# Three fixed expert pairs instead of two at the start of a mixture-of-experts layer

## The reference

```python
hid = silu(einsum('td,edf->tef', t, w_gate)) * einsum('td,edf->tef', t, w_up)
routed = einsum('tef,efd->td', hid * gates[:, :, None], w_down)
shared = (silu(t @ ws_gate) * (t @ ws_up)) @ ws_down
return (routed + shared).reshape(shp)
```

## Time and profile before

| What | Value |
|---|---|
| Time, median of 3 runs (lowest, highest) | 1366.26 us (1365.38, 1369.22) |
| The profiled execution: its time, its span | 1367.02 us, 1365.0 us |
| TensorE matmul busy | 1150.9 us, 84% of the span |
| VectorE, ScalarE busy | 441.6 us (32%), 301.1 us (22%) |
| Bytes moved, mean rate | 497.52 MB, 364 GB/s |
| Mean granted TensorE clock | 0.925 of full |

### The profile page before, as it was taken

One profiled execution on the slowest core, in us unless ns is written; L12 is line 12 of the kernel. 1 busy time (PEld: TensorE's weight loads), 2 busy tenths in 40 slices (PEclk: granted clock), 3 DMA queues, 4 the chain that ended last, 5 costly groups with the idle time before them and its releaser, 6 DMA issues.

```text
span 1365.0 us, 20661 instructions
## 1 busy us (share of the span) xinstructions
PE 1150.9 (84%) x7420; PEld 603.9 (44%) x7420; DVE 441.6 (32%) x1222; ACT 301.1 (22%) x562; POOL 69.3 (5%) x85
## 2 busy tenths in 40 slices
PE   3897988998888886978879998899977888887877
PEld 2675745444333432323348775544423333332323
DVE  0645474222122222212246474631222122212213
ACT  1523532111111111101144355111111111111102
POOL 0220010000000000000033002000000000000000
PEclk8899988999889888989989998999989898898989
DMA  9689586899999999999994947679999999999994
GB/s 364 251 330 399 212 341 247 352 412 421 419 418 417 416 406 422 405 421 420 418 400 143 358 161 309 222 318 413 421 419 416 420 416 415 412 421 420 420 421 166
DMA packets 95526, 497.52 MB, mean 364 GB/s; under 512 B 8752, under 2 KB 8752, under 8 KB 53744
## 3 DMA queue, kind: packets, MB, share of 16 engines
q1 hardware_dynamic: 93632, 491.48, 89.2%
q0 software_dynamic: 1840, 5.31, 1.0%
HBM read 494.14 MB, written 2.62 MB: 364 GB/s over the span
## 4 chain that ended last, share of the span: by engine, by line
PE 58%; DMA 30%; SPq 3%; issue 3%; ACT 2%; DVE 2%; POOL 1%; DVEq 1%; ACTq 0%
PE PS L1006 29%; DMA weights<-in_w_up 27%; PE PS L800 12%; PE PS L1038 4%; PE PS L974 3%; PE PS L945 2%; SPq L412 2%; PE PS L990 2%; DMA weights<-in_w_ada 2%; DMA weights<-in_w_in 1%; PE PS L821 1%; PE PS L967 1%; SPq L452 1%; PE PS L896 1%; PE PS L636 1%
## 5 line engine op out<-in xcount | busy, mean ns | idle before, releaser
L1006 PE MATMUL PS<-weights,gathered 128*32 128x512 f32 (+1 forms) x2624 | 408.9, 685 | 142.3 <-DMA weights<-in_w_up 134.4
L1006 PEld LDWEIGHTS PS<-weights,gathered 128*32 128x32 f32 (+1 forms) x2624 | 118.6, 130 | 428.9 <-issue 335.9
L1719 DVE SCALAR_TENSOR_TENSOR hidden<-PS,slot_gate,silu 128x256 f32<-128x256 f32 x50 | 24.2, 484 | 508.3 <-ACT silu L1254 506.2
L1038 PE MATMUL PS<-weights,hiddenT 128*32 128x512 f32 (+1 forms) x1312 | 182.3, 596 | 0.0
L1254 ACT ACTIVATE silu<-PS 128x256 f32<-128x256 f32 x50 | 19.2, 384 | 535.3 <-PE PS L1006 535.3
L974 PE MATMUL PS<-pick_rows,x_parts 128*128 128x384 f32 (+2 forms) x616 | 121.9, 348 | 6.6 <-DVE pick L1671 6.6
L974 PEld LDWEIGHTS PS<-pick_rows,x_parts 128*128 128x128 f32 x616 | 104.8, 195 | 49.1 <-issue 40.6
L800 PE MATMUL PS<-weights_split,hT_high 128*128 128x512 f32 x448 | 111.8, 405 | 8.1 <-ACT hT_high L1104 6.1
L1267 ACT ACTIVATE y_hi<-PS 128x512 fp32r<-128x512 f32 x100 | 59.7, 597 | 222.2 <-PE PS L1038 222.2
L800 PEld LDWEIGHTS PS<-weights_split,hT_high 128*128 128x128 f32 x448 | 86.0, 195 | 30.4 <-issue 11.8
L1730 DVE TENSOR_TENSOR y_lo<-PS,y_hi 128x512 fp32r<-128x512 f32 x100 | 69.2, 692 | 77.6 <-ACT y_hi L1267 77.6
(11 more groups left out here) (270 smaller groups left out, 912.7 us busy)
## 6 DMA issues: line engine op xcount, KB each, us to landing
weights<-in_w_down SPq DMA_DIRECT2D x128, 1024.0 KB, 11.8
weights<-in_w_gate SPq DMA_DIRECT2D x96, 1024.0 KB, 10.4
weights<-in_w_up SPq DMA_DIRECT2D x96, 1024.0 KB, 12.4
weights<-in_w_ada SPq DMA_DIRECT2D x24, 2048.0 KB, 13.3
weights<-in_w_gate SPq DMA_DIRECT2D x64, 512.0 KB, 7.0
weights<-in_w_up SPq DMA_DIRECT2D x64, 512.0 KB, 8.0
weights<-in_w_in SPq DMA_DIRECT2D x9, 2048.0 KB, 11.2
weights<-in_w_out SPq DMA_DIRECT2D x4, 2048.0 KB, 15.7
```

The costliest lines, as they stand in the source:

```text
L1006: last = mm(PS[a:z, 4, :].rearrange("p (a n) -> p a n", a=2), xgT[:, (b + 1) % 3, j, a:z], w[e][:, :, j, :], start=j == 0, stop=j == KT - ...
L1038: last = mm(PS[a:z, bank, :], hidT[:, j, a:z], w[e][:, j, n * HALF:(n + 1) * HALF], start=j == 0, stop=j == FT - 1, tile_position=(0, a), ...
```

## The change

A third pair, experts 4 and 5, is fixed and visited third, so that the hand-written visits are three TWO, two THREE and two TOP. The fixed experts' loads need no table. SyncE issues the loads of positions 4 to 15 pair by pair, and the wait for the table and the load of `ws_down` move behind the first pair's `w_gate` and `w_up` and `w_down`. Seven of the positions below 16 are halved instead of four. In visit 0, TensorE does `overflow_places`, `scatter_prep` (into bank 7) and `shared_hidden_out` behind step j = 1 and `items` behind j = 5; behind its products it gathers for the third pair alone (16 blocks of 128 columns), and visit 1 has 16 further blocks of 128 columns (`EXTRA`). `shared_down` goes behind the fourth visit. VectorE makes the third pair's picks ahead of the table, chooses for visit 3 alone after it, and reads the codes of visit 4 behind `hid` of visit 0.

```diff
...
-FIXED = 2
+FIXED = 3
+FIRST_FREE = 2 * FIXED
...
-VISITS = ((TWO, (0, 1)), (TWO, (2, 3)), (THREE, (4, 5, 6)), (THREE, (7, 8, 9)), (TOP, (10, 11)), (TOP, (12, 13)), (TWO, (14, 15)))
+VISITS = ((TWO, (0, 1)), (TWO, (2, 3)), (TWO, (4, 5)), (THREE, (6, 7, 8)), (THREE, (9, 10, 11)), (TOP, (12, 13)), (TOP, (14, 15)))
+SHARED_BEHIND = 3
+EXTRA = {0: ((2, (6,)),), 1: ((0, (0, 1, 2)), (2, (7,)))}
...
-HALVED, HALVED_AT = (4, 5, 8, 11), (4, 7)
-HALF_BY = {0: 1, 2: 2, 3: 3}
+HALVED, HALVED_AT = (4, 5, 6, 8, 9, 10, 13), (4, 7)
+HALF_BY = {0: 1, 1: 2, 2: 3, 3: 4, 4: 5}
...
+AT_FIRST = (((0, 1), 5), ((2, 3), 6), ((4, 5), 0), ((6, 7), 1))
...
                     load_expert(sp, l, 2 * b + 1, 2 * b + 1, ("w_down",))
-                sp.wait_ge(sht_mm, l + 1)
-                sp.wait_ge(table_ready, l + 1)
-                sp.dma_start(shared_down_w[:, :], rows(io["ws_down"][l])).then_inc(shared_in, 16)
...
-                    ns = VISITS[t][1]
-                    for n in ns:
-                        if n in (8, 11):
-                            sp.wait_ge(S["gu_half"], HALF_BY[user[n - 4]])
+                experts = {n: n for n in range(FIRST_FREE)}
+                for a in range(SLOTS, 16, 2):
+                    pair, loaded = (a, a + 1), []
+                    for n in pair:
+                        by = user[n - SLOTS]
+                        if halved(n):
+                            freed("gu_half", HALF_BY[by])
                             load_expert(sp, l, n, experts[n], ("w_gate", "w_up"), 0)
-                            freed("gu_mm", user[n - 4] + 1)
-                            load_expert(sp, l, n, experts[n], ("w_gate", "w_up"), 1)
-                        elif t > 2 or n == 6:
-                            freed("gu_mm", user[n - 4] + 1)
+                        elif by < user[a + 1 - SLOTS]:
+                            freed("gu_mm", by + 1)
                             load_expert(sp, l, n, experts[n], ("w_gate", "w_up"))
-                    if t + 1 < len(VISITS):
-                        after = {n: expert_of(n - 4) for n in VISITS[t + 1][1]}
-                    for n in ns:
-                        freed("down_mm", 2 * (user[n - 4] + 1))
+                            loaded.append(n)
+                    for n in pair:
+                        if n not in loaded:
+                            freed("gu_mm", user[n - SLOTS] + 1)
+                            load_expert(sp, l, n, experts[n], ("w_gate", "w_up"), 1 if halved(n) else None)
+                    if a == SLOTS:
+                        sp.wait_ge(table_ready, l + 1)
+                        sp.wait_ge(sht_mm, l + 1)
+                    if a + 2 < 16:
+                        experts.update({n: expert_of(n - FIRST_FREE) for n in (a + 2, a + 3)})
+                    else:
+                        last_round = sp.value_load(n_visits[0:1, 0:1], min_val=LAST_ROUND, max_val=MOST)
+                    for n in pair:
+                        freed("down_mm", 2 * (user[n - SLOTS] + 1))
                         load_expert(sp, l, n, experts[n], ("w_down",))
-                    experts = after
+                    if a == SLOTS:
+                        sp.dma_start(shared_down_w[:, :], rows(io["ws_down"][l])).then_inc(shared_in, 16)
 
                 with sp.Fori(FIRST_ROUND, last_round) as q:
...
                     if not first:
                         pe.wait_ge(S["xg_d"], t)
-                    pe.wait_ge(S["slots_done"], t + 1)
+                        pe.wait_ge(S["slots_done"], t + 1)
...
-                            if inside:
-                                inside()
+                        for work in inside.get(j, ()):
+                            work()
                     last.then_inc(S["gu_mm"], 1)
-                    pe.wait_ge(S["picked"], t + (AHEAD + 1))
+                    if first:
+                        pe.wait_ge(S["picked"], FIXED)
+                        pe.wait_ge(table_ready, l + 1)
+                    else:
+                        pe.wait_ge(S["picked"], t + (AHEAD + 1))
+                    if extra:
+                        pe.wait_ge(S["xg_x"], t)
+                        at = 0
+                        for u, js in extra:
+                            for j in js:
+                                last = gather(j, u, u + 1, 0, at)
+                                at += P
+                        last.then_inc(S["ga_x"], 1)
...
-                    else:
-                        for j in (6, 7):
-                            gather(j, 2, 3, 0, (j - 6) * P)
                     for j, bank, done in zip(GATHERED[(b + 1) % 3], (5, 6, 7), ("ga_a", "ga_d", "ga_c")):
-                        gather(j, 0, AHEAD, bank, 0).then_inc(S[done], 1)
+                        gather(j, FIXED - 1 if first else 0, AHEAD, bank, 0).then_inc(S[done], 1)
...
                     last.then_inc(S["ht_mm"], 1)
+                    if extra:
+                        pe.wait_ge(S["xg_x"], t + 1)
...
-                overflow_places()
-                pe.wait_ge(cleared, 2 * (l + 1))
-                scatter_prep(0)
-                shared_hidden_out()
+
+                def first_places():
+                    pe.wait_ge(cleared, 2 * (l + 1))
+                    scatter_prep(0, 7)
+                    shared_hidden_out()
+
+                in_first = {1: (overflow_places, first_places), 5: (items,)}
...
                 step(v.memset(visits[0:1, LIST:], NULL))
+                choose_fixed(2)
                 dve.wait_ge(item_mm, l + 1)
...
                 for t in range(FIXED, 4):
                     form, ns = visit_of(t)
-                    choose(t % 3, form, codes_of(ns[0] - 4, len(ns)))
-
-                def visit(q, b, following, form, position, n):
-
-
-                    codes = codes_of(position, n)
-                    t = of_round(q, 3, b + 1)
+                    choose(t % 3, form, codes_of(ns[0] - FIRST_FREE, len(ns)))
+
+                def visit(q, b, following, form, position, n, first=False):
+
+
+                    t, a = of_round(q, 3, b + 1), FIXED - 1 if first else 0
+                    if not first:
+                        codes = codes_of(position, n)
                     dve.wait_ge(S["silu_done"], t + 1)
                     dve.wait_ge(S["slots_done"], t + 1)
                     slot = (b + 1) % 3
                     v.scalar_tensor_tensor(hid[:, :], PS[:, 4, F:2 * F], slot_gate[:, slot:slot + 1], silu[:, :], ALU.mult, ALU.mult)\
                         .then_inc(S["hid_done"], 1)
+                    if first:
+                        codes = codes_of(position, n)
                     dve.wait_ge(S["ga_d"], t + 1)
```

More of the change, by code:

```diff
@@ L991, in scatter, with visit @@
                                    start=first and part == 0, stop=False, skip_group_check=True)
-                def visit(q, b, form, ns, loads, halves_out, inside=None):
+                def visit(q, b, form, ns, loads, halves_out, extra=(), inside={}):
                     t, tiles, first = of_round(q, 3, b + 1), TILES[form], q == -1 if type(q) is int else False
@@ L1055, in _ @@
                         pe.wait_ge(shT_ready, l + 1)
-                    visit(*round_of(t), form, ns, [(needed(n, 32), needed(n, 16)) for n in ns], t in HALF_BY, items if t == 0 else None)
-                    if t == 2:
+                    visit(*round_of(t), form, ns, [(needed(n, 32), needed(n, 16)) for n in ns], t in HALF_BY, EXTRA.get(t, ()),
+                          {} if t else in_first)
+                    if t == SHARED_BEHIND:
                         shared_down()
@@ L1243, in _ @@
                 act.wait_ge(act_step, l + 1)
-                for m, (js, bank) in enumerate((((0, 1, 2), 5), ((3, 4), 6), ((5, 6), 0), ((7,), 1))):
+                for m, (js, bank) in enumerate(AT_FIRST):
                     act.wait_ge(S["ga_a"], m + 1)
-                    last = gathered(js, 0, 1 if bank == 5 else 2, bank)
+                    last = gathered(js, 0, 2, bank)
                 last.then_inc(S["xg_a"], 1)
@@ L1621, in choose_fixed @@
                         .then_inc(S["picked"], 1)
-                for u in range(FIXED):
+                for u in range(2):
                     choose_fixed(u)
@@ L1673, in choose, with slots_of @@
                     last.then_inc(S["picked"], 1)
-                def slots_of(slot, form):
-                    placed = PS[:, 4, 0:NG * (P + PARTS)].rearrange("p (g c) -> p g c", g=NG)
+                def slots_of(slot, form, bank=4):
+                    placed = PS[:, bank, 0:NG * (P + PARTS)].rearrange("p (g c) -> p g c", g=NG)
                     v.tensor_copy(put[:, slot, :].rearrange("p (g t) -> p g t", g=NG), placed[:, :, PARTS:])
@@ L1733, in _ @@
                     form, ns = visit_of(t + 4)
-                    visit(*round_of(t), visit_of(t + 1)[0], form, ns[0] - 4, len(ns))
+                    visit(*round_of(t), visit_of(t + 1)[0], form, ns[0] - FIRST_FREE, len(ns), t == 0)
```

71 lines of the change are left out of this document (34 added, 37 removed).

## The result

The changed kernel takes 1370.3 us (median of 15 runs, 1367.3 to 1377.0) against 1365.4 for the kernel before in the same sessions. The ratio is 1.0034, 95% interval 1.0021 to 1.0048: slower, where 1361.5 was forecast. The profiled execution took 1368.61 us (span 1366.8), 1.6 above the profiled one of before.

The account below looks back on a forecast made before the run. The prediction took the stream of expert weights, about 420 GB/s, as the bound. Gains of 3.5 us in the first layer and 2.1 in the second took 1367.02 to 1361.4, stated as 1361.5, range 1355 to 1371.5.

Parts of the forecast that it names:

- the opening, step by step: First layer, first gathers to visit 2: products from 214.2 us, table at 221.45, visit 1 from 232.85, visit 2 ending at 263.5.
- half loads at no loss: Stream of weights: cutting 12 more loads per layer into 512 KB halves was taken to cost nothing in a full queue.
- there are 12 loads of 1 MB: Loads from the downs of positions 4 and 5 to position 8's second `w_up` half: 30.2 us, visit 3 at 265.0.
- a stop of some 2 to 3 us: Stream ahead of position 13's down load, which waits for visit 4; the load was to run from 303.8 us.
- 3.5 and 2.1: Forecast gains in us of the first and second layer's openings; 5.6 us together.
- A stop ahead of visit 3 of more than 3 us with the stream at work: One of the signs that would show the forecast wrong, given there as the sign of the halves.
- slow halves: Rival: half loads following each other run at 323 GB/s, 1.62 us each in place of 1.26; 1372.2 us, chance 0.19.
- the rival of the old wait: Rival in the opening: VectorE's register loads and the clock take all of the bound, visit 1 at 234.6; 1364.8 us, chance 0.20.
- no more: Experts of both layers: a changed start is worth only what it takes from the stream's standstill before 330 us.

## Why the prediction was wrong

**Right: the opening, step by step.** VectorE's timeline answers to the earlier trace rows.

```profile
214.56 0.42 DVE L1702 CAST put<-PS 128x256 fp32r<-128x256 f32 x1 [3.16 <-PE PS L985]
218.89 0.27 DVE L1728 TENSOR_SCALAR visits<-PS 1x122 int32<-1x122 f32 x1 [0.69 <-PE PS L941]
221.56 0.30 DVE L1692 TENSOR_TENSOR pick<-const,slot_of 128x128 bf16<-128x128 f32 x1 [2.40 <-issue]
222.72 0.48 DVE L1745 SCALAR_TENSOR_TENSOR hidden<-PS,slot_gate,silu 128x256 f32<-128x256 f32 x1
```

Measured from G, with the forecast in brackets: the first products at 4.6 (5.2), the table at 11.8 (12.5; before 9.4), `hid` at 15.4 (16.1 to 16.6), the down product at 17.6 (18.7), visit 1 at 23.0 (23.9). The down product took 5.35 at a granted clock of 0.68 from 224.97 to 230.32, where 3.58 + 1.6 was forecast. Visit 2 ended at 53.9 (54.5). Every step here came out within about 1 us.

**Right, as far as shown: half loads at no loss.** From 247.4 to 269.4 us, where 8's and 9's halves stand in a full queue, the stream ran at 418 GB/s, and cutting fewer changed nothing. The Trainium skill's wish for 1 MiB and more ("DMA: Bandwidth & Descriptors", section "Bandwidth"), named beside that rival and measured there with transfers issued from GpSimd, did not bear on these loads: 512 KB behind other loads ran at the full rate, and what looked like the cost of 10's and 13's halves was a queue with too little in it. The halves of position 6, which came through at about 240 to 246 us, are a case apart (352 GB/s, with the DMA engines busy for 0.98 of the time). For them, and for those of 4 and 5 at the start, where both kernels limp, no run decides.

**Wrong: "there are 12 loads of 1 MB" at 2.52 us up to visit 3, and from there only "a stop of some 2 to 3 us".** Three terms failed.

- Visit 3 started at G+58.0, 2.0 after the forecast 56.0. From the landing of 4's down (235.2) to that of position 8's last half (265.2) the 11 loads took 30.0 us, 2.73 each and not 2.52. The stretch from 238 to 246 us at 366 GB/s, not 416, is 1.0 of these 2.3 us; its cause and the rest stay open.
- With visit 2 ending 0.6 early, that made TensorE's wait 4.09 us in place of 1.5 (263.5 to 265.0), and the products behind it took 8.77 at a granted clock of 0.81, in place of the 7.0 in the visit's 15.1. I had priced such a slow start only inside a rival.
- So visit 4 ended at G+97.0 against 93.3, and position 13's down ran from about G+99 in place of 94.8. It landed at 309.5, G+102.1; in the kernel before at 312.0, G+103.0. (The prediction had reckoned its start there at G+98.3, by that landing some 2 us too early.) So 0.9 us is left of the 3.5 that were forecast for the first layer. By the table the layers gained -0.2 and 1.2 of stream, not 3.5 and 2.1.

Up to visit 7's `hidden` the first layer gained 0.1 and 0.0 us, the second 2.1 and 2.5. The second's 2.1 thus came out in the number, by luck and not by its terms: the stop forecast at 2 to 3 us cost 6.0 there.

The error under these is one of method. I followed two loads, 8's and 13's down, and took the stream between them for fed. Counted as SyncE can issue them, 11 loads were let go in 35 us, so any lateness of visit 3 passed straight on. "A stop ahead of visit 3 of more than 3 us with the stream at work" was named as a sign of slow halves; it came (4.09 us, the stream at 418 GB/s), and not from slow halves of 8 and 9: with 8 alone in its turn, in place of sharing it with 9, visit 3 came 2.4 us earlier. Slow halves of position 6 are not excluded; what the slow stretch there cost is 1.0 us. Nor was it the rival of the old wait, since VectorE and the clock cost what was forecast for them.

**Not foreseen: the rounds.** The prediction said that a change to the start is worth what it takes from the stream's stops there, "no more", and so put the rounds at nothing. In the profiles they cost 3.9 and 5.1 us more. With the 2.2 and 2.6 us gained up to visit 7 and the stretches outside, the changed kernel's profiled executions are 1.6 and 2.1 us longer. The medians differ by 4.9 and 5.5: both profiled executions of the changed kernel lie below its median (by 1.7 and 2.9 us), and where the other 3 us lie no profile shows. That most of the difference goes when TensorE is kept busy in the rounds is shown by the times. Why this opening leaves fewer short rounds is not: two profiles per kernel are few, and I have no row that leads from the one to the other. It stays open.

## What to carry to other kernels

When a stop of a load queue is removed, list every load that follows with the event that lets it go, and compare what each stretch hands out with what the stream can take; a gain that is spent again 40 us later shows only there. A visit that needs three loads should have them in the order it needs them: with 8 before 9 the same change gained 6 us on the kernel before instead of losing 5, and with 14 ahead of 13's down 11.6. A load may be pulled ahead of one that waits, but only by as much as the waiting one has to spare: 2 MB ahead of 13's down filled a hole, 4 MB moved the wait to TensorE. The two were tried in different kernels, the 2 MB with 8 first, so how much of that is the size alone is not shown.

## What the runs showed of the hardware

- A wait of TensorE can have a price behind it, and its length alone does not set it. After 1.62 us the next 64 products took 7.07 us at a granted clock of 1.00; after 4.09 us 8.77 at 0.81; after 5.78 and 5.13 us 9.05 and 9.86 at 0.78 and 0.71, a part of them at the lower level of 1.2 GHz. Between these both come: 8.77 after 1.98 us in the kernel before, and 7.07 after 3.01 us in the changed kernel's second layer:

```profile
920.54 3.01 issue
923.56 7.07 PE PS L1009 x64
```

The same visit of the first layer, in the two profiles of the changed kernel, waited equally long and went on at 0.81 in the one and at 1.00 in the other. What decides it is not shown.

```profile
320.89 8.72 PE L1009 MATMUL PS<-weights,gathered 128*32 128x512 f32 x64 [2.22 <-issue]
321.53 7.07 PE L1009 MATMUL PS<-weights,gathered 128*32 128x512 f32 x64 [2.23 <-issue]
```

- A stream that runs at 330 GB/s over 38 us need not be one of slow transfers. With whole loads the same stretch showed 91 GB/s, then 411, then 176, and the same sum.
